# A mixture-of-experts stage on one core: the index of an expert's V row, made before or after the next row's dot product

## What is computed

```
def block(xt):                                    # 128 tokens at a time, two blocks
    q = (xt @ w_query).reshape(TOKEN_BLOCK, PEER_HEADS, 2, PEER_HALF)
    s = jnp.einsum('thpd,hpnd->thpn', q, sub_keys)
    s_top, i_top = lax.top_k(s, K)                # K = 16
    cand = ...sums of the two halves' best...     # 256 candidates
    best, pos = lax.top_k(cand, K)
    idx = jnp.take_along_axis(cand_idx, pos, axis=-1)
    g = jax.nn.softmax(best, axis=-1)
    u = expert_u[idx]
    v = expert_v[idx]
    act = jax.nn.gelu(jnp.einsum('td,thkd->thk', xt, u))
    return jnp.einsum('thk,thkd->td', (g * act), v)
```

## Time and profile before

| | us |
|---|---|
| three runs | 1457.02, 1458.49, 1459.40 |
| median of the runs | 1458.49 |
| the profiled execution | 1459.09 |
| its span (first to last instruction) | 1457.5 |

### The profile page before, as it was taken

One profiled execution on the slowest core, in us unless ns is written; L12 is line 12 of the kernel. 1 busy time (PEld: TensorE's weight loads), 2 busy tenths in 40 slices (PEclk: granted clock), 3 DMA queues, 4 the chain that ended last, 5 costly groups with the idle time before them and its releaser, 6 DMA issues.

```text
span 1457.5 us, 25909 instructions
## 1 busy us (share of the span) xinstructions
PE 1373.4 (94%) x8512; PEld 1067.3 (73%) x8512; DVE 1150.3 (79%) x2772; ACT 785.1 (54%) x1768; POOL 499.1 (34%) x600
## 2 busy tenths in 40 slices
PE   9999999999999999999999999999898998888878
PEld 9898999999989999998998985444454433333333
DVE  7777788878878888678799779887777778778764
ACT  6656544456556444456885535455555454455443
POOL 1111011110110111010111026776667676767672
PEclk9999999999999999999999999999999999999999
DMA  9999999999999999999999959999999999999997
GB/s 365 342 352 334 350 413 389 400 390 357 349 351 357 370 396 400 378 386 344 339 346 339 349 191 362 402 408 399 403 396 410 396 404 409 392 401 406 401 409 308
DMA packets 141598, 542.73 MB, mean 372 GB/s; under 512 B 22654, under 2 KB 22798, under 8 KB 128064
## 3 DMA queue, kind: packets, MB, share of 16 engines
q0 software_dynamic: 101904, 396.41, 72.3%
q1 hardware_dynamic: 38880, 141.92, 25.7%
q10 hardware_dynamic: 720, 3.24, 0.6%
HBM read 576.08 MB, written 135.27 MB: 488 GB/s over the span
## 4 chain that ended last, share of the span: by engine, by line
PE 60%; DMA 17%; DVE 11%; ACT 4%; issue 4%; POOL 4%; POOLq 0%; DVEq 0%; ACTq 0%
PE PS L757 10%; PE PS L748 10%; PE PS L740 10%; DMA late<-expert_uv,idx 8%; DMA attn<-expert_uv,idx 6%; PE PS L1288 5%; PE PS L788 3%; PE PS L1004 3%; PE PS L1000 3%; PE PS L1005 3%; PE PS L891 3%; DVE late L2596 2%; DVE attn L2596 2%; DMA attn<-expert_u,idx 2%; PE PS L1239 2%
## 5 line engine op out<-in xcount | busy, mean ns | idle before, releaser
L1398 ACT ACTIVATE early_splits<-ring 128x1024 fp32r<-128x1024 f32 x166 | 175.1, 1056 | 128.2 <-PE PS L748 99.2
L1856 DVE TENSOR_TENSOR early_splits<-ring,early_splits 128x1024 fp32r<-128x1024 f32 x166 | 202.5, 1221 | 32.9 <-ACT early_splits L1398 32.7
L1762 ACT ACTIVATE gel<-dot,token_rms 128x1 f32<-128x1 f32 x256 | 75.2, 294 | 255.4 <-DVE dot L2596 253.6
L2596 DVE CUSTOM_DVE_ANT_0 late<-late,PS 128x1024 f32<-128x1024 f32 x125 | 151.8, 1215 | 58.8 <-DMA late<-expert_uv,idx 58.5
L2596 DVE CUSTOM_DVE_ANT_0 attn<-attn,PS 128x1024 f32<-128x1024 f32 x125 | 151.9, 1215 | 35.6 <-DMA attn<-expert_uv,idx 29.3
L1288 PE MATMUL PS<-late,wrg 128*128 128x512 f32 x284 | 133.7, 598 | 19.2 <-ACT wrg L1754 19.0
L1288 PE MATMUL PS<-attn,wrg 128*128 128x512 f32 x288 | 133.8, 595 | 6.8 <-ACT wrg L1754 5.7
L1331 PE MATMUL PS<-late,wrg 128*128 128x512 f32 x208 | 103.3, 621 | 32.8 <-ACT wrg L1754 32.7
L672 POOL DMA_INDIRECT attn<-expert_u,idx x93 | 87.6, 942 | 98.9 <-DVE idx L2548 70.4
L682 POOL DMA_INDIRECT attn<-expert_v,idx_v x93 | 93.0, 1000 | 72.6 <-issue 26.3
L1288 PEld LDWEIGHTS PS<-late,wrg 128*128 128x128 f32 x284 | 51.2, 190 | 87.8 <-issue 87.6
(11 more groups left out here) (467 smaller groups left out, 3368.5 us busy)
## 6 DMA issues: line engine op xcount, KB each, us to landing
ring<-wstream SPq DMA_DIRECT2D x256, 512.0 KB, 9.0
expert_uv<-expert_u POOLq DMA_DIRECT2D x64, 1024.0 KB, 15.0
expert_uv<-expert_v POOLq DMA_DIRECT2D x64, 1024.0 KB, 15.0
ada<-w_ada POOLq DMA_DIRECT2D x32, 512.0 KB, 10.3
late<-w_ada POOLq DMA_DIRECT2D x16, 512.0 KB, 11.7
late<-wstream SPq DMA_DIRECT2D x4, 512.0 KB, 10.6
attn<-expert_u,idx POOLq DMA_INDIRECT x93, 8.6
attn<-expert_v,idx_v POOLq DMA_INDIRECT x93, 7.7
```

The lines of the kernel that those rows point to most:

```text
L1398: act.activation(hi_of(u), raw(u), ACT.Copy).then_inc(hi_ready, 1)
L1856: ve.tensor_tensor(lo_of(u), raw(u), hi_of(u).bitcast(F32), ALU.subtract).then_inc(units_begun, 1)
L2596: ve.tensor_tensor_reduce(row, row, H2N[n // 8], 1.0, 0.0, ALU.mult, ALU.add, dot[:, n % 2, k:k + 1]).then_inc(dot_ready, 1)
```

## The change

The pick of a row moves in VectorE's queue from behind the next row's dot to the end of its own row's step, behind the row's dot and its step of top-k (and behind `probabilities`, where that runs). Nothing else is moved; every instruction is there as often as before.

```
--- before.py
+++ after.py
@@ -2630,8 +2630,6 @@
                     ve.wait_ge(h2_ready, 2 * (n // 8 + 1))
                 for k in range(EXPK):
                     row_dot(n * EXPK + k)
-                    if n or k:
-                        pick_row(n * EXPK + k - 1)
                     if n == 0 and k == 0:
                         for q in range(6):
                             decode(0, q, slice(8, EXPK))
@@ -2651,6 +2649,7 @@
                                          ALU.mult).then_inc(g2diag, one(g2diag))
                     if k == (6 if n else 14) and n + 1 < GROUPS:
                         probabilities(n + 1)
+                    pick_row(n * EXPK + k)
                     if n == 9 and k == 8:
                         ve.wait_ge(took["act"], FINAL_TAKEN)
                         ve.wait_ge(row_used, weighed_by[last_weighed[0]])
```

## The result

The changed kernel is slower: a median of 1483.71 us in five runs (1482.95 to 1487.94) against 1458.49 (1456.99 to 1462.52), a ratio of 1.0168, 95% interval 1.0154 to 1.0182. That is 25.2 us, where 4.4 were forecast. The profiled execution has a span of 1483.0 us. What follows is read in it.

The account below looks back on a forecast made before the run. The prediction took the full DMA engines to bound groups 1 to 14; 2.75 us in group 0, 1.15 in groups 2 to 4 and 0.5 in group 5 made 4.4 over 1458.49, forecast 1463 us, range 1457.5 to 1469.

Parts of the forecast that it names:

- The start's 2.75 us: Group 0: new waits make V 0.13 2.75 us late, all carried on into the full stretch.
- VectorE as a whole: Full groups: VectorE needs 34.8 us with 5.2 of new waits, below the DMA's 36.06; cost nothing.
- the cover is 1.3 us a group: Full groups: the room left to VectorE for making up its new waits, 1.3 us a group.
- Groups 2 to 4: Late dot 4 makes GpSimd stand 1.25 us longer; 0.45, 0.05 and 0.65 us lost, sum 1.15.
- from group 6 on ... nothing is lost: From group 6 on row 12 lands after 8.4 to 10.3 us, which covers the 1.25 us; cost nothing.
- These gave 1.65 us: Forecast loss after group 0: 1.15 us in groups 2 to 4 and 0.5 in group 5.
- VectorE becomes the bound: Rival: each of ten picks a group costs 0.3 us more, VectorE needs 37.8 us a group; 1481 us, chance 0.06.
- Its sign, 37 us in groups 6 to 13: Groups 6 to 13 taking 37 us each, not 36, would show that VectorE binds.
- The queue hides it: Rival: DMA engines still have 1 to 1.5 us of work behind the stops; 1459.8 or 1458.5 us, chance 0.30.
- the V's come earlier: Rival: picks done 0.5 to 1.9 us sooner release GpSimd and fill the DMA dips; 1455.5 us, chance 0.06.
- a landing of 6.7 us: Least time from issue to landing of a joint row, 6.7 us, taken as that of an empty DMA queue.

Follow-up runs that it names:

- the run of group 0 alone: The kernel before, with the picks moved as in the change in group 0 only, groups 1 to 15 as before: 1460.98 us, ratio 1.0012.
- before, six products: The kernel before, with six small products of zeros in TensorE's queue ahead of weighing rows 4 (and 12 from group 9 on): 1458.93 us, ratio 1.0001.
- after, six products: The changed kernel, with six small products of zeros in TensorE's queue ahead of weighing rows 4 (and 12 from group 9 on): 1472.59 us, ratio 1.0097.
- the delayed dot 4 above: The kernel before, picks unmoved, with three extra VectorE operations between dot 3 and dot 4 of groups 1 to 14: 1480.03 us, ratio 1.0144.
- row 3's was taken out: The changed kernel, with the pick of row 3 (row 11 in group 0) put back behind the next dot: 1460.74 us, ratio 1.0011.
- two operations of VectorE: The kernel before, picks unmoved, with two extra VectorE operations (2.2 us) between dot 3 and dot 4: 1463.35 us, ratio 1.0021.
- twelve: Twelve products of zeros ahead of weighing rows 4 and 12: changed kernel 1479.90 us, ratio 1.0125; kernel before 1470.16 us, ratio 1.0067.

## Why the prediction was wrong

**What held.** Durations and places: the pick of row 3 6.28 us behind dot 2, waits for weights of 5.2 us a group, dot 0.12 at 899.62 (899.15 forecast) and V 0.13 at 908.48 (907.8), with a stage that began 0.38 us later. The start's 2.75 us is within what the run of group 0 alone gave. The finding that a pick is not what releases V held as well: in the changed kernel four V's of 155 went out right behind their pick, nine before.

**The step that failed** is the one that followed a late dot 4 through groups 1 to 14: in "VectorE as a whole" it is "late in rows 4 to 8" and "on time again at row 9 or 12. Cost on this account: nothing; the cover is 1.3 us a group"; in "Groups 2 to 4" it makes GpSimd's stop longer by 1.25 us and no more, and "from group 6 on ... nothing is lost". These gave 1.65 us; the rows give 21.4. Two things were wrong in it.

*A late row was carried on as late and nothing else.* It had TensorE weigh row 4 in the time of before. In the changed kernel TensorE stands for 2.1 to 3.2 us ahead of row 4 in eleven groups (0.9 to 1.9 in the same ones before), and in eight of them its clock is at the lower level for a part of what follows, so that row 4 takes 2.5 to 3.75 us in place of 1.96. No term of the sum stood for this. It is 11.8 us of the 21.4 by the profiled sums (21.4 less 9.6), 10.4 by the runs. By the runs it is also half of what a late dot 4 costs without a moved pick.

*The cover was taken too large and the lateness too small.* The loop through the slot of row 4 can be cut into pieces, here summed over groups 1 to 13 in the order of time (us):

| from, to | before | after | before, six products | after, six products |
|---|---|---|---|---|
| dot 4 to issue of V 5 | 107.5 | 114.4 | 111.7 | 104.6 |
| V 5 to issue of row 12 | 16.9 | 16.9 | 17.0 | 16.9 |
| issue of row 12 to dot 12 | 112.7 | 99.4 | 111.2 | 104.3 |
| dot 12 to issue of the next row 4 | 118.6 | 125.1 | 118.6 | 121.9 |
| its issue to its dot | 115.2 | 136.0 | 112.5 | 133.1 |

The last line is what the pick does: 1.6 us a group, not 1.25. From dot 1 to dot 4 it is 6.71 us before and 8.32 after, in the mean of groups 1 to 14; the prediction's own rows, 6.1 to 7.3 and 7.95 to 8.4, have their middles 1.5 apart, so its 1.25 was too low by them already. With the clock held (the two right columns) the first and third lines give 7.1 + 6.9 us back, 1.1 a group and not 1.3, and the fourth takes 3.3. What is left of 20.7 is 6.7, and with the 3.3 it is 10.0 us. Without (the two left ones), the first line takes 6.9 instead of giving 7.1, the third gives 13.3 and the fourth takes 6.5: the first is mainly the clock's place. The table says where the time goes; that the lateness of dot 4 is its cause is shown by the delayed dot 4 above, and the split into lateness and cover is worked out, not tried. To set a lateness against a cover was right; 1.25 against 1.3 came out at nothing, 1.6 against 1.1 is half a microsecond in each of 13 groups.

**The rivals.** *VectorE becomes the bound* had 1481 us, near the result, and its mechanism is not the one: each pick cost what I took, VectorE's busy time is 29.4 us of 37.6 a group, and 30 us of its waits cost nothing when row 3's was taken out. What settles it is the run with six products: VectorE waits there for weights as long as in the changed kernel (53.5 us between 1060 and 1445 us, 54.0 without the products), and its groups are 11.4 us shorter. Its sign, 37 us in groups 6 to 13, did appear (298.4 us in eight groups), from another cause. *The queue hides it* is refuted by 0.59 and 0.21 of DMA share; *the V's come earlier* by the stops.

**Left open.** Why a stop of 2.58 us was followed by the lower clock and one of 2.98 us in another group was not. And how the clock's 10 to 12 us split further, since its late weighings also make the next row late.

## What to carry to other kernels

A full share of the DMA engines over a group does not mean that lateness is covered: follow the loop from a dot through weighing, buffer and issue to the dot that needs it, and ask what is left in that loop, not in the engine's sum. A wait moved onto an in-order queue should be judged at its longest instance, not by its total: seven waits of 0.4 us a group were free, and one of 2.4 to 2.6 us cost nearly everything. When TensorE is made to wait longer in a stage where it is nearly full, look at its granted clock, and try a few products of zeros that fit into the stop: six cost nothing here, and tell the clock from the lateness; twelve were longer than the stop and cost 0.67%.

## What the hardware showed that I had not expected

Short stops of TensorE were enough for the lower clock: behind 3.16 us in group 4 it was 0.67 and then 0.50, and the weighing of row 4 took 3.33 us instead of 1.96; behind 2.58 us in group 3 it was 0.50 as well, between 999 and 1001 us. Ahead of row 4 of group 14, a stop of 2.98 us left it up (1.98 us). In the kernel before, whose stops ahead of row 4 are 1.9 us or less, none of these weighings was slow. Other runs show it behind as little: 1.88 us in group 12 with two operations of VectorE (3.13 us), 1.93 in group 11 with the change in group 0 alone (3.34). So the length of this stop alone does not tell whether the clock falls.

The shortest joint gather took 6.4 us from issue to landing in the changed kernel (6.7 in the earlier trace rows) and 5.5 in it with six products, so a landing of 6.7 us was not yet that of an empty queue. The prediction took it for one; a shorter time would have left more cover behind the stops, so this is not what made the forecast too low.
